# Prompt indexer: the first product of both chains, and the causal mask, move from DVE to Pool; four buffers of clipped scores in place of three

## The reference

```python
s = jnp.einsum('bthd,bsd->bths', qi, ki)             # 16 heads of 64
score = jnp.einsum('bths,bth->bts', jax.nn.relu(s), wi)
causal = key_pos[None, :] <= q_pos[:, None]
score = jnp.where(causal[None], score, -jnp.inf)
_, sel = lax.top_k(score, topk)                      # topk = 256
```

## Time and profile before

| what | value |
|---|---|
| time, median of 3 runs | 1539.3 us (1537.16 to 1541.38) |
| the profiled execution's own time | 1535.68 us |
| its span, first to last instruction | 1533.7 us |
| its mean granted TensorE clock | 0.977 |
| PE busy | 1423.2 us, 93% |
| DVE busy | 1187.9 us, 77% |
| POOL busy | 791.8 us, 52% |
| ACT busy | 675.6 us, 44% |

### The profile page before, as it was taken

How to read it: one execution, slowest core, us unless ns; L and a number is a source line. 1 busy time by engine, 2 the same in 40 slices (tenths; PEclk the granted TensorE clock), 3 DMA queues, 4 the chain that set the end, 5 groups by cost and what they waited for, 6 DMA issues and landing times.

```text
span 1533.7 us, 30661 instructions
## 1 busy us (share of the span) xinstructions
PE 1423.2 (93%) x10257; PEld 1300.5 (85%) x10257; DVE 1187.9 (77%) x2220; ACT 675.6 (44%) x1275; POOL 791.8 (52%) x872
## 2 busy tenths in 40 slices
PE   4999998878996878889999999999998999999999
PEld 4998776636874556689998999999998999999999
DVE  6799989999985896643587777677889776777775
ACT  4200147856444765652243434443444434444432
POOL 4633211050257951234266675776668766766673
PEclk9999999989996999999999999999999999999999
DMA  7303100130144443142023223333223333332222
GB/s 221 90 28 100 47 28 15 28 86 11 58 163 131 125 118 108 32 158 97 1 75 105 82 89 96 103 100 99 90 84 97 98 118 112 99 106 88 82 82 72
DMA packets 97216, 135.01 MB, mean 88 GB/s; under 512 B 15233, under 2 KB 51329, under 8 KB 96991
## 3 DMA queue, kind: packets, MB, share of 16 engines
q1 hardware_dynamic: 94514, 131.17, 27.2%
q10 hardware_dynamic: 2613, 2.70, 0.5%
HBM read 121.17 MB, written 13.02 MB: 87 GB/s over the span
## 4 chain that ended last, share of the span: by engine, by line
PE 49%; issue 16%; POOL 15%; DVE 14%; ACT 4%; DMA 1%; POOLq 0%; DVEq 0%; ACTq 0%
POOL w_lo L1158 15%; PE ps L1197 14%; PE ps L1198 14%; PE ps L1199 14%; DVE mcnt L2645 2%; PE ps L1513 1%; PE ps L1527 1%; DVE qi_tok L2587 1%; ACT rl L1945 1%; DVE y L2525 1%; PE ps L1497 1%; DVE sm L2817 1%; DVE acc L2578 1%; DVE acc L2587 1%; DVE left L2613 1%
## 5 line engine op out<-in xcount | busy, mean ns | idle before, releaser
L1197 PE MATMUL ps<-hi_t,w_hi 128*128 128x272 f32 (+4 forms) x1672 | 496.9, 297 | 3.0 <-POOL w_lo L1158 2.6
L1198 PE MATMUL ps<-lo_t,w_hi 128*128 128x272 f32 (+4 forms) x1672 | 495.3, 296 | 0.0
L1199 PE MATMUL ps<-hi_t,w_lo 128*128 128x272 f32 (+4 forms) x1672 | 495.0, 296 | 0.0
L1197 PEld LDWEIGHTS ps<-hi_t,w_hi 128*128 128x128 f32 (+1 forms) x1672 | 314.3, 188 | 5.2 <-POOL w_lo L1158 3.0
L1198 PEld LDWEIGHTS ps<-lo_t,w_hi 128*128 128x128 f32 (+1 forms) x1672 | 314.3, 188 | 0.6
L1199 PEld LDWEIGHTS ps<-hi_t,w_lo 128*128 128x128 f32 (+1 forms) x1672 | 314.3, 188 | 0.5
L1158 POOL TENSOR_TENSOR w_lo<-w_raw,w_hi 128x256 fp32r<-128x256 f32 x264 | 201.0, 783 | 152.0 <-ACT w_hi L2256 150.6
L1158 POOL TENSOR_TENSOR w_lo<-raw_up,w_hi 128x256 fp32r<-128x256 f32 x264 | 216.9, 844 | 114.4 <-ACT w_hi L2256 114.2
L1197 PE MATMUL ps<-f_hi,w_hi 128*128 128x272 f32 x704 | 206.6, 294 | 8.1 <-DVE x L3137 7.3
L1199 PE MATMUL ps<-f_hi,w_lo 128*128 128x272 f32 x704 | 204.0, 290 | 0.0
L1198 PE MATMUL ps<-f_lo,w_hi 128*128 128x272 f32 x704 | 203.8, 289 | 0.0
(11 more groups left out here) (381 smaller groups left out, 2765.5 us busy)
## 6 DMA issues: line engine op xcount, KB each, us to landing
raw_up<-in_w_up SPq DMA_DIRECT2D x88, 256.0 KB, 3.0
w_raw<-in_w_gate SPq DMA_DIRECT2D x88, 256.0 KB, 2.7
w_f<-in_w_down SPq DMA_DIRECT2D x88, 256.0 KB, 2.8
w_raw<-in_w_in SPq DMA_DIRECT2D x16, 512.0 KB, 3.7
kt_b<-in_cache_kt SPq DMA_DIRECT2D x48, 128.0 KB, 2.4
v_b<-in_cache_v SPq DMA_DIRECT2D x48, 128.0 KB, 2.3
x<-in_x_t SPq DMA_DIRECT2D x8, 544.0 KB, 8.1
w_raw<-in_w_u SPq DMA_DIRECT2D x8, 512.0 KB, 3.8
```

Source lines behind the costliest of these rows:

```text
L1197: pe.matmul(out, a_hi, b_hi, start=first, stop=False)
L1198: pe.matmul(out, a_hi, b_lo, start=False, stop=False)
L1199: return pe.matmul(out, a_lo, b_hi, start=False, stop=last)
```

## The change

Pool makes `begun[0]` = relu of head 0 times its weight, `begun[1]` = relu of head 1 times its weight, and adds the causal mask to the last 128 keys of `begun[0]` (a third instruction). DVE starts at head 2, and reads `begun` as what is added to in heads 2 and 3. L2578, L2579 and L2583 go. In Pool's list the three instructions of tile i stand ahead of the low parts of the queries of tile i+1. The ring of relus has four buffers, and ACT waits for head n-4: for the count of Pool (`begun_done`) where that was head 0 or 1, else for `acc_done`. PE's transposes stand after heads 7 and 11, ACT's copies after heads 8 and 12. DVE's count per tile is 15, not 17. The semaphore `q_zero` is given up for the new one, and its four uses go to `consts_made`, with counts raised by two. The hunks left out are those, and places where NI + 1 becomes TILE_SUMS.

```diff
@@ -200,9 +200,12 @@
 
     return sum((j + 1) * P for j in range(FIRST, t))
 
+POOL_HEADS = 2
+TILE_SUMS = NI - POOL_HEADS + 1
+
 def added(n):
 
-    return n // NI * (NI + 1) + n % NI + 1
+    return n // NI * TILE_SUMS + n % NI - POOL_HEADS + 1
 
 def dve_parts(n):
 
@@ -350,7 +353,8 @@
         rl_new = at("rl_new", 70176, [P, SR])
         rl_s = [rl[:, 0, :], rl[:, 1, :], at("rl_s2", 16384, [P, PAST]), at("rl_s3", 20480, [P, PAST])]
         sacc_odd = at("sacc_odd", 16384, [SR, SKEYS])
-        rl3 = [rl[:, 0, :], rl[:, 1, :], at_w("rl_2", 12288, [P, S])]
+        rl4 = [rl[:, 0, :], rl[:, 1, :], at_w("rl_2", 12288, [P, S]), at_w("rl_3", 16384, [P, S])]
+        begun = at_w("begun", 28672, [P, POOL_HEADS, S])
         kiw = at("kiw", 71200, [P, NT, KIW])
         kis_t = [at(f"kis_t{i}", 4096 * i, [P, PAST]) for i in range(NS // 2)]
         qis_t = at("qis_t", 4096 * NSEL, [P, NS, NI, TS])
@@ -803,7 +807,7 @@
 
             for b in range(NS):
                 page = page_numbers(sp, b)
-                sp.wait_ge(acc_done, (b // 2 + 2) * (NI + 1))
+                sp.wait_ge(acc_done, (b // 2 + 2) * TILE_SUMS)
                 for j in range(NPG):
                     sp.dma_start(kis_t[b // 2][half_of(b), j * PAGE:(j + 1) * PAGE],
                                  A["cache_it"][bass.ds(page[j], 1)].rearrange("o d s -> d (o s)")
@@ -1032,11 +1036,34 @@
             pool.wait_ge(kit_ps, 1)
             pool.wait_ge(ki_out, 32)
             pool.memset(w_all[:, :, :], 0.0).then_inc(consts_made, 1)
-            for i in range(NSEL):
+
+            def index_query_lows(i):
+
                 pool.wait_ge(qs_hi, i + 1)
                 pool.tensor_tensor(qs_tok[:, :, ID:], qi_tok[:, i, :].rearrange("p (h d) -> p h d", d=ID),
                                    qs_tok[:, :, 0:ID].bitcast(F32), ALU.subtract).then_inc(qs_lo, 1)
-            pool.wait_ge(acc_done, NSEL * (NI + 1))
+
+            def begin_sums(i):
+
+                t = FIRST + i
+                own, keys = t * P, (t + 1) * P
+                for h in range(POOL_HEADS):
+                    n = i * NI + h
+                    pool.wait_ge(relu_done, n + 1)
+                    if i > 0:
+                        pool.wait_ge(acc_done, added((i - 1) * NI + POOL_HEADS + h))
+                    pool.tensor_scalar(begun[:, h, 0:keys], rl4[n % 4][:, 0:keys], wi_tok[:, t, h:h + 1], None, ALU.mult
+                                       ).then_inc(begun_done, 1)
+                pool.wait_ge(begun_done, 3 * i + 1)
+                pool.tensor_tensor(begun[:, 0, own:keys], begun[:, 0, own:keys], kf[:, K_TRI:K_TRI + P], ALU.add
+                                   ).then_inc(begun_done, 1)
+
+            index_query_lows(0)
+            for i in range(NSEL):
+                begin_sums(i)
+                if i + 1 < NSEL:
+                    index_query_lows(i + 1)
+            pool.wait_ge(acc_done, NSEL * TILE_SUMS)
             for n in range(17, 25):
                 split(n)
             key_inverses()
@@ -1415,8 +1442,8 @@
                         pe.matmul(out, qs_t[i % 2][:, h, :], ki_hh[:, a:a + w], start=True, stop=False)
                         mm = pe.matmul(out, qs_t[i % 2][:, h, :], ki_ll[:, a:a + w], start=False, stop=True)
                     mm.then_inc(idx_mm, 1)
-                    if h in (5, 10) and i + 1 < NSEL:
-                        index_transposes(i + 1, h // 10)
+                    if h in (7, 11) and i + 1 < NSEL:
+                        index_transposes(i + 1, h // 11)
 
             pe.wait_ge(qit_ready, 2 * NSEL)
             for h in range(NI):
@@ -1940,14 +1967,18 @@
                 for h in range(NI):
                     n = i * NI + h
                     act.wait_ge(idx_mm, n + 1)
-                    if n >= 3:
-                        act.wait_ge(acc_done, added(n - 3))
-                    act.activation(rl3[n % 3][:, 0:keys], wide(2 * (n % 3), keys), ACT.Relu).then_inc(relu_done, 1)
+                    if n >= 4:
+                        j, x = divmod(n - 4, NI)
+                        if x < POOL_HEADS:
+                            act.wait_ge(begun_done, 3 * j + x + 1)
+                        else:
+                            act.wait_ge(acc_done, added(n - 4))
+                    act.activation(rl4[n % 4][:, 0:keys], wide(2 * (n % 3), keys), ACT.Relu).then_inc(relu_done, 1)
                     if i + 1 < NSEL:
                         if h == 0:
                             split_index_queries(i + 1)
-                        if h in (6, 11):
-                            take_index_queries(i + 1, h // 11)
+                        if h in (8, 12):
+                            take_index_queries(i + 1, h // 12)
 
             act.wait_ge(qist_ps, 1)
             for odd in range(2):
@@ -2569,22 +2600,22 @@
                 t = FIRST + i
                 a0, keys = acc_at(t), (t + 1) * P
                 even, odd = acc[:, a0:a0 + keys], qi_tok[:, i, 0:keys]
-                for h in range(NI):
+                for h in range(POOL_HEADS, NI):
                     n = i * NI + h
                     dve.wait_ge(relu_done, n + 1)
                     w = wi_tok[:, t, h:h + 1]
-                    src = rl3[n % 3]
-                    if h == 0:
-                        dve.tensor_scalar(acc[:, a0:a0 + t * P], src[:, 0:t * P], w, None, ALU.mult)
-                        dve.scalar_tensor_tensor(acc[:, a0 + t * P:a0 + keys], src[:, t * P:keys], w,
-                                                 kf[:, K_TRI:K_TRI + P], ALU.mult, ALU.add).then_inc(acc_done, 1)
-                    elif h == 1:
+                    src = rl4[n % 4]
+                    mine = odd if h % 2 else even
+                    if h == POOL_HEADS:
+                        dve.wait_ge(begun_done, 3 * i + 3)
+                    if h == POOL_HEADS + 1:
                         dve.wait_ge(qs_lo, i + 1)
-                        dve.tensor_scalar(odd, src[:, 0:keys], w, None, ALU.mult).then_inc(acc_done, 1)
+                    if h < 2 * POOL_HEADS:
+                        so_far = begun[:, h - POOL_HEADS, 0:keys]
                     else:
-                        mine = odd if h % 2 else even
                         dve.wait_ge(acc_done, added(n - 2))
-                        dve.scalar_tensor_tensor(mine, src[:, 0:keys], w, mine, ALU.mult, ALU.add).then_inc(acc_done, 1)
+                        so_far = mine
+                    dve.scalar_tensor_tensor(mine, src[:, 0:keys], w, so_far, ALU.mult, ALU.add).then_inc(acc_done, 1)
                 dve.wait_ge(acc_done, added(i * NI + NI - 1))
                 dve.tensor_tensor(even, even, odd, ALU.add).then_inc(acc_done, 1)
             dve.memset(s_lo[:, :], 0.0)
```

More of the change, by code:

```diff
@@ L500, in decoder_program @@
         kt_lo = sem("kt_lo")
-        q_zero = sem("q_zero")
+        begun_done = sem("begun_done")
         masks_ready = sem("masks_ready")
@@ L1052, in _ @@
                     other = slice((1 - kh) * HD, (2 - kh) * HD)
-                    pool.memset(q_st[other, b, 1, kh].bitcast(F32), 0.0).then_inc(q_zero, 1)
+                    pool.memset(q_st[other, b, 1, kh].bitcast(F32), 0.0).then_inc(consts_made, 1)
                 if b == 0:
-                    pool.wait_ge(q_zero, 2)
+                    pool.wait_ge(consts_made, 4)
                     query_inverses(LATE_QUERY)
                     pool.wait_ge(head_rs, LATE_QUERY + 2)
-            pool.wait_ge(q_zero, 4)
+            pool.wait_ge(consts_made, 6)
             query_inverses(LATE_QUERY + 1)
@@ L1480, in scores @@
                     pe.wait_ge(kt_lo, NKV)
-                    pe.wait_ge(q_zero, 2)
+                    pe.wait_ge(consts_made, 4)
                 if n == NH:
-                    pe.wait_ge(q_zero, 4)
+                    pe.wait_ge(consts_made, 6)
                 if h == 0:
@@ L1959, in _ @@
                 ins.then_inc(qist_ready, 1)
-            act.wait_ge(acc_done, NSEL * (NI + 1))
+            act.wait_ge(acc_done, NSEL * TILE_SUMS)
             act.wait_ge(snew_mm, 1)
@@ L2594, in _ @@
                                    -1.0, None, ALU.mult))
-            dve.wait_ge(acc_done, NSEL * (NI + 1))
+            dve.wait_ge(acc_done, NSEL * TILE_SUMS)
             def take_sample_scores():
```

## The result

| | kernel before | changed kernel |
|---|---|---|
| median of 4 runs | 1540.1 us | 1553.7 us (1552.8 to 1555.6) |
| ratio | | 1.0097, 95% interval 1.0083 to 1.0110 |
| profiled execution | 1535.7 us, span 1533.7 | 1554.3 us, span 1552.5 |

The account below looks back on a forecast made before the run. DVE was taken to bound the six tiles. Pool's stalls of 9.3 against 7.2 shed (+2.1), the buffer -2.5 and the boundary +2.0 made +1.6 us, on 1539.3: 1540.9, with 8 in 10 for 1534.5 to 1551.

Parts of the forecast that it names:

- What bounds the kernel, and that a us here goes through: Six tiles before the choice: DVE sets the time, least in small tiles; a us gained or lost reaches the end.
- DVE sheds 7.2 us: Six tiles: DVE loses 18 instructions, twelve products at 5.6 us and six masked pieces at 1.6.
- What Pool holds up, 9.3 us: Six tiles: DVE stalls beside Pool's new work, 7.7 us for twelve products and 1.6 for six mask adds.
- The fourth buffer, -2.5 us: DVE's waits for ACT's relus, 3.7 us, mostly vanish with four buffers and moved transposes; range 0 to -3.7.
- The boundary, +2 us: Tile starts: DVE's head 2 waits for Pool's products and mask, in small tiles only, none from tile 3; 0.5 to 6.
- B: Slower rival: Pool's product runs at its subtraction's pace, 17.7 us of DVE for the products; 1551 us, chance 0.18.
- C: Rival: the wait at head 2 shows at all five boundaries, 1.3 us each, by lost turns; 1545 us, chance 0.15.
- A: Faster rival: Pool's product does not hold DVE up, which pays only for mask adds; 1532 us, chance 0.10.
- The marks that I set for the changed profile: Signs expected in the new trace, among them Pool's 1024-key products at 1.0 to 1.3 us, or 2.4 for B.

## Why the prediction was wrong, by its own steps

**What bounds the kernel, and that a us here goes through:** right. The stage grew by 15.0 us, and the medians by 13.6. In the profiled pair the choice took another 2.9 us. DVE instructions with two inputs there run into Pool's subtractions of 2.4 us, not the same ones in the two traces. Of the small ones, five took above 0.8 us in the kernel before and seven after, 4.8 us more in sum, and a longer one took 2.0 less. One of the seven is

```profile
402.72 2.37 DVE L2688 TENSOR_TENSOR s_add<-s_few,s_w 128x7 f32<-128x7 f32 x1
```

**DVE sheds 7.2 us:** right. The run with short products, which has next to nothing in place of the 18 instructions, has a stage shorter by 4.2 us, with 3.4 us more of idle time of DVE in it.

**What Pool holds up, 9.3 us:** right for the extra work with the low parts first (7 to 8 us by the medians, 8.7 by the lengths of DVE's instructions). In the changed kernel itself DVE's instructions grew by only 2.5 us, 0.37 to 0.80 at each sum, since the second product runs while DVE waits anyway. So this term was 7 us too high there, and offset a part of the boundary's miss.

**The fourth buffer, -2.5 us:** right alone (-2.5 of waits). In the changed kernel it came to nothing, 3.7 us of waiting as before: the low parts stood behind Pool's products in its list, and PE waited 13.0 us for them (2.5 before). With the low parts on DVE the 3.7 are 0.7. That queue was named in the prediction only ahead of DVE's head 2, not ahead of PE.

**The boundary, +2 us: this step failed.** It measured +19.8 (16.7 and 3.1). I had one number for Pool's product, 0.8 to 1.0 us per 1024 keys, taken from how long a rounding held DVE up, and used it as the time until the product is ready. Ready it is after 2.8. Two in a row and a mask of 0.45 are 6 us, where DVE has two adds and a sum left, 3.3 us at 896 keys. The rest is Pool's own waiting: at each boundary the first product was longer than the second, which DVE's adds didn't disturb, by 0 to 1.57 us, 3.2 of the 16.7 in all. From tile 3 on the products did begin under heads 14 and 15 of the tile before, as I had it, but they were not done in time. So the sentence that none of this shows from tile 3 on had the slope the wrong way: the wait is longest in the widest tile. ACT's lead doesn't help beyond that, for head 0's relu can't be written before head 12 of the tile before is added.

**The rivals.** B's time, 1551, came nearest. It had Pool's pace about right (2.8 us, where it said 2.35), but drew the wrong cost from it: it let Pool's product hold DVE for 2.15 us per 1024, and it held it for 0.78. That its time is near is luck. C had the place right, the row of products ahead of head 2 in every tile, and gave it 1.3 us a boundary by lost turns. It was 3.3: 0.6 on average by lost turns, the rest by the products' own length. A is out, as Pool's product does hold a DVE add up, by 0.78 us. The range ended at 1551 because no case joined B's slow product with C's place. The marks that I set for the changed profile contained it: products of 1.0 to 1.3 us, or 2.4.

**The Trainium skill.** That Pool and a DVE instruction with two SBUF inputs contend (SBUF — State Buffer, Who interferes with whom), the runs bear out. That the first holds the ports to its instruction's end they don't: beside Pool's product of 2.8 us DVE lost 0.78, and the tap in the earlier trace rows that began 0.02 us ahead of Pool's subtraction was the one that took 2.22 us more. The Trainium skill's price of about 1.03 cycles per element for a one-input loop (GPSIMD Engine Reference, 3.1 Elementwise — side-by-side cycle accounting), an estimate of 0.88 us, is nearer the rounding's 1.04 and the copy's 1.3 than the product's 2.8.

**Open:** why `tensor_scalar` on Pool takes longer than the two-input form and holds DVE for a fraction of it. The trace has no view inside a Pool instruction.

## What to carry to other kernels

For a step moved to another engine, price two things apart: how long it disturbs the old engine, and how long until its result is ready; then lay the second along the list of what waits for it, in the widest tile too. Ask of each instruction behind it in the new engine's list who waits for that one: with Pool's extra work ahead of the low parts, DVE lost 10 us by waiting down that chain, nearly the 11 by which Pool held it up. And the gain was in the opposite move: Pool's one subtraction held DVE up by 2.1 us a tile, and DVE does it in 1.2. It paid only with PE's transposes moved later, after heads 7 and 11.

## What of the hardware was not expected

- Pool's `tensor_scalar` over 128x1024 f32 takes 2.8 us, by a constant or by a number per partition; its two-input product with one input repeated 2.14; its rounding 1.04. At 384 keys the first takes 1.26 us. These are times beside an idle or little disturbed DVE; beside DVE's adds of 896 and 1024 keys the first took 4.4 to 5.0.
- They lengthen a concurrent `scalar_tensor_tensor` of DVE by 0.78, 1.64 and 0.79 us, so the longest of them holds DVE up no more than the shortest.
